# Three rounded TensorE passes for the mixers' input and output projections, over weights and rows that are split into two parts on the core

## The reference, cut to what matters

```python
for l in range(DEPTH):                       # DEPTH = 2
    h = _rmsnorm(x, g_mix[l])                # x: 256 x 1024
    z = h @ w_in[l]                          # 1024 x 2724: the input projection
    (cq, ckv, kr, q_b, k_b, v_b, q_c, k_c, v_c, f_c, q_d, k_d, v_d) = jnp.split(z, offsets, axis=-1)
    y_a = _mla(...); y_b = _dilated_attention(...); y_c = _forgetting_attention(...)
    y_d = _differential_attention(...)       # each 256 x 256
    y = jnp.concatenate([y_a, y_b, y_c, y_d], axis=-1)
    x = x + y @ w_out[l]                     # 1024 x 1024: the output projection
    h = _rmsnorm(x, g_ffn[l])
    x = x + (_swiglu(h, ...) if l % 2 == 0 else _moe(h, ...))
return _rmsnorm(x, g_final)
```

## Time and profile before

| | before |
|---|---|
| median of 3 runs | 1492.8 us |
| the profiled execution | 1492.25 us |
| its span, first to last instruction | 1490.5 us |
| TensorE busy, share of the span | 97% |
| mixer of layer 0, TensorE | 14.6 to 161.3 us of the span |
| dense part | 169.7 to 359.7 us |
| mixer of layer 1 | 362.9 to 509.3 us |
| experts | from 528.5 us |

### The profile page before, as it was taken

How to read it: one execution, slowest core, us unless ns; L and a number is a source line. 1 busy time by engine, 2 the same in 40 slices (tenths; PEclk the granted TensorE clock), 3 DMA queues, 4 the chain that set the end, 5 groups by cost and what they waited for, 6 DMA issues and landing times.

```text
span 1490.5 us, 17754 instructions
## 1 busy us (share of the span) xinstructions
PE 1448.9 (97%) x6915; PEld 1149.1 (77%) x6915; DVE 1126.2 (76%) x1210; ACT 951.8 (64%) x1153; POOL 67.7 (5%) x87
## 2 busy tenths in 40 slices
PE   7999899999999999999999999999999999999997
PEld 3556699997556578888888888888888888888885
DVE  3543454543554489998999999999999999899996
ACT  1422444432233268888888888888888888888885
POOL 1110000000010120000000000000000000000000
PEclk9999999999999899999999999999999999999999
DMA  9821454344622389999999999999999999999970
GB/s 312 324 86 57 170 193 175 113 149 170 225 100 71 137 320 375 371 366 395 383 371 394 386 371 385 389 377 374 392 364 376 392 387 368 393 376 376 394 295 30
DMA packets 187207, 435.19 MB, mean 292 GB/s; under 512 B 7822, under 2 KB 14580, under 8 KB 187124
## 3 DMA queue, kind: packets, MB, share of 16 engines
q1 hardware_dynamic: 183556, 421.93, 76.7%
q0 software_dynamic: 3136, 10.54, 2.5%
q10 hardware_dynamic: 432, 1.57, 0.3%
HBM read 426.66 MB, written 7.37 MB: 291 GB/s over the span
## 4 chain that ended last, share of the span: by engine, by line
PE 96%; DVE 2%; DMA 1%; ACT 1%; issue 1%; SPq 0%; POOL 0%; POOLq 0%; ACTq 0%
PE ps L1692 74%; PE ps L1493 10%; PE ps L1507 4%; PE ps L1783 2%; PE ps L1562 1%; PE ps L1527 1%; PE ps L1543 1%; DMA ring<-in_w_in 1%; DVE wideT L1169 0%; PE ps L1758 0%; PE ps L1748 0%; PE ps L1589 0%; PE ps L1465 0%; PE ps L1733 0%; PE ps L1827 0%
## 5 line engine op out<-in xcount | busy, mean ns | idle before, releaser
L1218 DVE TENSOR_TENSOR split<-ring,split 128x1024 fp32r<-128x1024 f32 x738 | 889.8, 1223 | 154.6 <-ACT split L854 84.1
L865 ACT ACTIVATE split<-ring 128x1024 fp32r<-128x1024 f32 x672 | 710.4, 1062 | 170.7 <-PE ps L1692 169.7
L1692 PE MATMUL ps<-split,hTs 128*128 128x512 f32 x2688 | 625.1, 391 | 2.0 <-DVE hTs L1218 2.0
L1692 PEld LDWEIGHTS ps<-split,hTs 128*128 128x128 f32 x2688 | 500.9, 188 | 105.7 <-DVE hTs L1218 2.1
L1692 PE MATMUL ps<-split,acts 128*128 128x512 f32 x1608 | 376.0, 390 | 1.5 <-DVE acts L1218 1.5
L1692 PEld LDWEIGHTS ps<-split,acts 128*128 128x128 f32 x1608 | 300.9, 188 | 64.0 <-DVE acts L1218 1.9
L1493 PE MATMUL ps<-ring,hT 128*128 128x512 f32 (+2 forms) x384 | 152.2, 553 | 2.3 <-DMA ring<-in_w_in 2.1
L1692 PE MATMUL ps<-hTs,split 128*128 128x256 f32 x1056 | 128.9, 285 | 2.2 <-DVE hTs L1218 2.2
L1692 PEld LDWEIGHTS ps<-hTs,split 128*128 128x128 f32 x1056 | 128.6, 194 | 2.9 <-DVE hTs L1218 2.6
L1493 PEld LDWEIGHTS ps<-ring,hT 128*128 128x128 f32 x384 | 73.0, 193 | 71.0 <-issue 66.3
L854 ACT ACTIVATE split<-ring 128x1024 fp32r<-128x1024 f32 x66 | 69.4, 1057 | 91.1 <-PE ps L1692 91.1
(11 more groups left out here) (187 smaller groups left out, 612.5 us busy)
## 6 DMA issues: line engine op xcount, KB each, us to landing
ring<-in_w_exp_gate SPq DMA_DIRECT2D x56, 2048.0 KB, 10.3
ring<-in_w_exp_up SPq DMA_DIRECT2D x56, 2048.0 KB, 10.3
ring<-in_w_exp_down SPq DMA_DIRECT2D x56, 2048.0 KB, 10.8
ring<-in_w_in SPq DMA_DIRECT2D x8, 2048.0 KB, 9.6
ring<-in_w_ffn_gate SPq DMA_DIRECT2D x5, 2048.0 KB, 7.8
ring<-in_w_ffn_up SPq DMA_DIRECT2D x5, 2048.0 KB, 9.2
ring<-in_w_ffn_down SPq DMA_DIRECT2D x5, 2048.0 KB, 7.8
ring<-in_w_out SPq DMA_DIRECT2D x4, 2048.0 KB, 11.8
```

The costliest lines, as they stand in the source:

```text
L865: act.activation(ex_unit(v)[0], ex_part(c, u), ACT.Copy).then_inc(hi_done, 1)
L1218: dve.tensor_tensor(dst, src, high.bitcast(F32), ALU.subtract).then_inc(signal, 1)
L1692: ins = pe.matmul(dst, a[ia], b[ib], start=(first and i == 0), stop=(last and i == 2))
```

## The change

The Z and W steps work on units as the feed-forward stages do. A unit is two k-slices of a chunk (up to 128 x 1024 values), 24 units for Z and 8 for W in each mixer. A step such as Z30 is now the first two units of chunk 3 for both token tiles, no longer one tile for all k; Z31 is the other two. Each unit is twelve matmuls (two tiles, two slices, three passes). At each Z or W step ScalarE and VectorE first split the units of the step after it (`mixer_high`, `mixer_low`), before their other work of that step. The rows of h are split into `hTs`, those of y into `yTs` (the same memory), the high part on ScalarE, the low part on VectorE. `unit_done`, `hi_done` and `lo_done` count mixer units too; `chunk_done` is gone.

`split` and `hTs` now live through the mixers. To make room, the ring is cut in two: `ring_a` with four slots, and `ring_b` with three slots in memory that the mixers use, so a load into it waits for `y_done` = 9, the end of the attention. `slot_plan` fixes which chunk goes to which slot. LM is moved ahead of QD; both `rope_d` are at Z20, `latents` at Z10, the rotation after LM at Z21; the steps WB, H0, H1 become W2, W3, W4. Of a mixer's first and last steps the order is new, too: units of Z00 are split in `norm_in` and `norm_T`, and `norm` splits two units of the dense part between the two tiles instead of one.

```diff
-MIXER = ["Z00", "Z01", "Z10", "Z11", "LT", "Z20", "QD", "LM", "J0", "Z21", "Z30", "J1", "F1", "Z31", "J2",
+MIXER = ["Z00", "Z01", "Z10", "Z11", "LT", "Z20", "LM", "QD", "J0", "Z21", "Z30", "J1", "F1", "Z31", "J2",
...
-         "W0", "J8", "W1", "YB", "J9", "WB", "H0", "J10", "H1", "YC"]
+         "W0", "J8", "W1", "YB", "J9", "W2", "J10", "W3", "YC", "W4"]
+RING_A = 4
+FF_SLOTS = (1, 2, 4, 5, 6, 3, 0)
+EX_SLOTS = (2, 3, 4, 5, 6, 0, 1)
+M1_SLOTS = (1, 2, 3, 0)
...
+                if k >= RING_A and not any(m >= (FF_AT if l == 0 else EX_AT) for m in before):
+                    sp.wait_ge(y_done[l], NJ)
...
+            def mixer_high(l, step):
+                for j in STEP_UNITS[step]:
+                    v = mixer_unit(l, j)
+                    n, _, wid, src = mixer_part(l, j)
+                    act.wait_ge(slot_in[chunk_slot(n)], landed[n])
+                    if v >= UNITS:
+                        act.wait_ge(unit_done, v + 1 - UNITS)
+                    act.activation(as_block(ex_unit(v, 2 * wid)[0], 2), src, ACT.Copy).then_inc(hi_done, 1)
...
+                    if step[0] in "ZW" and step != Z_STEPS[-1]:
+                        after = Z_STEPS[Z_STEPS.index(step) + 1]
...
+                            mixer_high(l, after)
+                    if step[0] == "Z" and step[2] == "1":
+                        for t in range(TILES):
+                            z_chunk(int(step[1]), t)
...
+                def z_unit(j):
+                    c, u = divmod(j, 4)
+                    ks, wid, parts = mixer_parts(j)
...
+                    for t in range(TILES):
+                        if j == 0:
+                            pe.wait_ge(hTl_done, 4 * 2 * l + 2 * t + 2)
+                        elif u == 0:
+                            pe.wait_ge(z_done[l], 2 * (c - 1) + t + 1)
+                        for i, k in enumerate(ks):
+                            ins = three(ps[:, t, 0:wid], [hTs[:, p, k, t * P:(t + 1) * P] for p in range(2)],
+                                        [p[:, i, :] for p in parts], k == 0, k == KC - 1)
```

More of the change, by code:

```diff
@@ L1007, in norm_T, with mixer_low @@
                                       ALU.mult).then_inc(hT_done, 1)
+            def mixer_low(l, step):
+                for j in STEP_UNITS[step]:
+                    v = mixer_unit(l, j)
+                    _, _, wid, src = mixer_part(l, j)
+                    high, lo = ex_unit(v, 2 * wid)
+                    dve.wait_ge(hi_done, v + 1)
+                    low(as_block(lo, 2), src, as_block(high, 2), lo_done)
             def rope(v, n, half, t):
@@ L1144, in mixer @@
                         latents()
+                    elif step == "Z11" and l == 0:
+                        lambdas()
                     elif step == "LT":
@@ L1150, in mixer @@
                                               ALU.mult).then_inc(bt_done[l], 1)
-                    elif step == "Z10":
-                        rope_d(0)
                     elif step == "Z20":
-                        rope_d(1)
-                    elif step == "LM":
+                        for t in range(TILES):
+                            rope_d(t)
+                    elif step == "Z21":
                         for t in range(TILES):
@@ L1428, in _ @@
             dve.wait_ge(g_done, 1)
+            for l in range(DEPTH):
+                a = GAIN_AT["g_diff_sub"] + l
+                ins = dve.tensor_scalar(g_sub[:, l:l + 1], g_cols[:, a:a + 1], 1.0 - (0.8 - 0.6 * math.exp(-0.3 * l)), None,
+                                        ALU.mult)
+            ins.then_inc(g_done, 1)
             for l in range(DEPTH):
@@ L1469, in arrived, with three @@
             def arrived(n):
-                pe.wait_ge(slot_in[n % RING], landed[n])
+                pe.wait_ge(slot_in[chunk_slot(n)], landed[n])
+            def three(dst, a, b, first, last):
+                for i, (ia, ib) in enumerate(((0, 0), (0, 1), (1, 0))):
+                    ins = pe.matmul(dst, a[ia], b[ib], start=(first and i == 0), stop=(last and i == 2))
+                return ins
             def mixer(l):
@@ L1492, in z_chunk @@
-                    for k in range(KC):
-                        ins = pe.matmul(ps[:, t, 0:wid], hT[:, k, t * P:(t + 1) * P], w_c[:, k, :],
-                                        start=(k == 0), stop=(k == KC - 1))
-                    ins.then_inc(chunk_done if t else z_ps[l], 1)
+                    for t in range(TILES):
+                        if j == 0:
[5 more added lines that the diff above has]
+                                        [p[:, i, :] for p in parts], k == 0, k == KC - 1)
+                        if u == 3 and t == 0:
+                            ins.then_inc(z_ps[l], 1)
@@ L1682, in mixer @@
                             transposed(k - 1, 1)
-                for t in range(TILES):
-                    pe.wait_ge(bt_done[l], BATCH["YC"][t] + 1)
-                    for h in range(2):
-                        y_times_w(h, t, (4, 5)).then_inc(chunk_done if t else w_ps[l], 1)
-            def three(dst, a, b, first, last):
-                for i, (ia, ib) in enumerate(((0, 0), (0, 1), (1, 0))):
-                    ins = pe.matmul(dst, a[ia], b[ib], start=(first and i == 0), stop=(last and i == 2))
-                return ins
             def dense_ff():
-                pe.wait_ge(hTl_done, 4)
+                pe.wait_ge(hTl_done, 8)
                 for kind, s in ff_order(FF_STEPS):
```

347 lines of the change are left out of this document (224 added, 123 removed).

## The result

The changed kernel took **1509.1 us** (median of four, 1507.9 to 1510.3) and the kernel before 1493.5 beside it: the ratio is 1.011 (95%: 1.0097 to 1.0122), slower by 15.6 us. The forecast was 1494 with a range up to 1506, so it was 15 us too low, and its range ended 3 us short. Two executions in all, one of the kernel before (2112 us) and one of an experiment (1817 us), ran at a much lower granted clock throughout; medians and ratios leave them out. The profiled execution has a span of 1506.0 us, against 1490.5.

A forecast was written before the change was run, and what follows sets the result against it. The prediction took TensorE, busy 97% of the span, as the bound. Cheaper passes saving 37.4 us against 37.3 of new waits, plus 2 for the clock, took 1492.25 to 1494 us, range 1481 to 1506.

The forecast's parts named there:

- The experts' own code is unchanged: Experts' stage, behind the mixers: code unchanged, so costed at nothing.
- rival C: Loads into ring_b arrive late at the dense part or the experts: up to 10 us, 1504; chance 0.05.
- The clock: Both mixers: a fall to the slow clock behind new stalls costs 1.1 to 2.0 us; 2 us added in all.
- J1's wait: Each mixer: scores ready at T+14.7, job 0's combination at T+16.1, so TensorE stalls 1.4 us.
- rival B: TensorE runs at half rate after three long waits a mixer, 2.0 us each: 1504; chance 0.22.
- Z30 starts: Each mixer: splits behind J0's exponentials free Z30 at T+8.4 (T: end of J0's scores); stall 5.5 us.
- J2's wait: Each mixer: TensorE ready at T+23.0, job 1's combination, behind low parts, done at T+28.3; stall 5.3 us.
- layer 1: first matmuls: Start of layer 1's mixer: TensorE starts 3 us later and stops once more for 1.6, 4.6 us together.
- The savings: Mixer projections: three cheaper passes, 24 matmuls of 512 columns in 5.58 us; 18.7 us saved a mixer, 37.4 in all.
- Rival D: Mixers' 512-wide steps: a rounded pass costs 0.215 us, not 0.2325; 8 us less, 1486; chance 0.07.
- Rival A: Attention's latency in the mixers is hidden, only the starts cost (9 us): 28 saved, 1464; chance 0.07.
- its half: One of the two stalls of 5 us gone in each mixer: 1483; chance 0.12.

The follow-up runs named there:

- The filled runs: The changed kernel with acts moved 32 or 96 bytes, plus unread matmuls in TensorE's two idle stretches of each mixer: 1496.8 and 1491.5 us.
- the better order: The aligned version with ScalarE issuing high parts ahead of a beat's exponentials and evacuating Z2 ahead of J0's: 1477.6 us.
- the filled, aligned run: The aligned version plus unread matmuls in TensorE's two idle stretches of each mixer: 1491.5 us, ratio 0.9994 to the kernel before.
- the aligned version: The changed kernel with 96 bytes of padding, so acts lies a multiple of 128 bytes from split: 1501.7 us.

## Why the prediction was wrong, point by point

**"The experts' own code is unchanged", costed at nothing: the step that failed most.** The forecast put the stages behind the mixers at no change. The instructions are the same, but an operand of theirs moved. 1608 matmuls by 6.3 ns are 10.1 us, and the run that moves `acts` alone in the kernel before costs 9.9. The diff gave what was needed to see it, since it moves `split` and `hTs`, but nothing in the trace before shows that the distance between two operands has a price. The forecast's own sign for this, longer experts, stood under rival C, the late loads; whoever had gone by it alone would have looked for the cause in the ring.

**The clock, 2 us in the sum: mis-sized.** The filled runs give 7.3 and 10.2 for what hangs on the two waits of each mixer. The kernel after itself was not filled. An estimate for it from its chain is about 9: the 24 matmuls behind the four waits took 7.39, 7.39, 8.17 and 7.76 us, which is 8.7 over 5.5 each; the small matmuls ahead of Z40 add 1.2 in each mixer; and 1.15 a mixer goes off again, J1's wait, which is there with the filling and gone without. The forecast priced a fall at 1.1 to 2.0 and let most of them be absorbed. The mechanism was right, down to its place: the loss behind Z30 was largely taken out of J1's stall. That was also rival B. Its price doesn't add up as written: three waits of 2.0 in two mixers are 12 in all, which gives its 1504, while 12 more than the forecast's 2 would be 1506. Its 1504 came nearest, with C's; it failed to reach 1509 because it held no placement. By the Trainium skill (TensorE: Matmul & The Clock Gate, "HAM oscillation — how this bites in real kernels") idle gaps between bursts bring the slow clock back; the two filled runs agree.

**The waits: right in place, and nearly in size.**

| term, layer 0 unless named | forecast | measured |
|---|---|---|
| first high and low of Z00 | 1.9 | 2.0 |
| Z30 starts | T+8.4 | T+8.3 |
| J1's wait | 1.4, less by the slow clock | 0; 1.15 with the filling |
| J2's wait | T+23.0 to T+28.3 | T+23.0 to T+29.3 |
| QD | 1.0 | 1.0 |
| last matmul by w_out to the dense part | 10.9 | 11.0 |
| layer 1: first matmuls | 3 later, and a stop of 1.6 | 2.8 later, and a stop of 0.6 |

The smaller terms, for QA and for Y, were not looked up one by one. The last but one is from TensorE's timeline (its last matmul by w_out ends at 160.5, the dense part starts at 171.5). J2's wait is a microsecond longer than the walk gave, because the combination takes 3.3 us instead of 2.4. The timelines of VectorE and of GpSimd show it; VectorE:

```profile
74.78 1.63 DVE L1229 TENSOR_TENSOR E<-E,row_inv 128x1024 f32<-128x1024 f32 x1
76.44 1.02 DVE L1231 TENSOR_TENSOR E<-E 128x512 f32<-128x512 f32 x1
```

and GpSimd:

```profile
75.29 1.62 POOL L711 TENSOR_TENSOR hn<-z,const 128x256 f32<-128x256 f32 x1
76.87 1.11 POOL L712 TENSOR_TENSOR hn<-z,const 128x256 f32<-128x256 f32 x1
```

L1231 takes 1.02 us here and took 0.69 before; GpSimd's rotation, which used to run at another time with 0.64 for the same product, takes 1.62. Both are longer only where they run side by side, in both layers. The Trainium skill (GPSIMD Engine Reference, "1. Specifications") says that GpSimd shares its SBUF interfaces with VectorE, with contention when a VectorE instruction has two SBUF inputs; the rows agree, but no run here took one of the two away, so this cause is argued, not shown.

**The savings: right for the passes.** The passes cost 5.47 to 5.55 us for 24 at full clock, against 5.58 in the forecast. Rival D, the rule by which they would cost 5.16, fell with that.

**Rival C fell, though one of its signs came up.** TensorE waits for no DMA behind the first load, and the experts start 19.5 us after the last matmul by w_out in layer 1 (before: 19.2).

**Rival A fell for this kernel, and its half is near what the better order does.** The forecast's 1483 was "one of the two stalls gone in each mixer"; with Z30's cut to 0.7 and J2's to 0.1 it is 1477.6. A's condition, a latency that is hidden, needed another order on ScalarE than the one the diff writes.

**The sum.** Placement 10.1, clock about 9 (both from the times of matmuls), and so, of the measured 15.6, 3 to 4 us in the kernel's favour for the savings against the waits (the filled, aligned run makes it about 5). The forecast had 0, 2 and 0.1. The ledger was thus too low by 3 to 5 us, which hid a part of the other two errors: by luck the miss is 15 us and not 18 or more. Some of it can be named. The passes are up to 0.1 cheaper a step, layer 1's stop is a microsecond shorter, and the kernel before had a 512-wide step of 8.02 in layer 1 that the forecast counted at 6.87; against that, J2's wait is a microsecond longer in each mixer. The rest was not traced.

What stays open: why the aligned version has slower mixers than the kernel after. It reaches the dense part at 174.4 and the experts after 173.3 us, against 171.5 and 170.7, in profiles of kernels that differ only in 96 bytes. The traces show where most of it goes. Z41 in the chain of work, first of the kernel after, then of the aligned version:

```profile
94.80 5.55 PE ps L1638 x24
```

```profile
96.54 7.40 PE ps L1639 x24
```

From 96 to 100 us the granted clock is 1.00 in the first and 0.50 in the second. It falls once more there, ahead of Z41, in layer 1 too, although in layer 0 TensorE was equally busy just before in both (2.79 us from 88 to 92 and 2.78 from 92 to 96). So the placement came out as 7.4 by the medians, 10.1 by the matmuls' own times and 11.7 by the two stages whose code is the same. What sets the places at which the clock falls was not tried.

## What to carry to other kernels

When a change moves a buffer, its neighbours' instructions are part of the change: list the distances between the operands of the hot matmuls before and after, and compare the mean time of a group whose code is untouched first. A pass that is cheaper on the bounding engine pays only if its preparation is issued ahead of the long latency chain on the helper engines; here the same work in the other order on ScalarE was worth 24 us, with the clock's part in it. A wait of 5 to 6 us in a stretch of matmuls cost more than its own length: the 24 matmuls behind it took 1.9 to 2.7 us more.

## What the runs showed of the hardware

The time of an fp32r matmul of 512 moving columns depends on the distance between its stationary and its moving operand. 24 of them take 5.61 us at a multiple of 128 bytes, 5.67 at 64 more, 5.76 at 32 more. Moving both operands alike changes nothing, and matmuls of 256 moving columns with the two operands' tiles exchanged didn't show it. Unused bytes between two tiles moved a kernel of 1493 us by 9.9 us, and by 24.8 where two stationary operands were off. And matmuls whose result nobody reads can be worth their issue: 42 of them in each mixer gave back 7.3 us in one version and 10.2 in another.
